# Delta rule: the products of the inverse's first levels as 64x64 blocks in two corners of the array, with their waits one projection matmul earlier

## The chip, the cores and the metric

The kernel runs on one core of a Trainium2 chip. The metric is the device time of one execution in microseconds (us), the median of a few runs. Before the change it is 1946.24 us over 3 runs (1946.16 to 1946.36).

## The reference

Two transformer blocks on a sequence of 512 positions with 2048 channels, in float32. The first block has three branches (a gated MLP with spatial gating, a gated delta rule, cross attention on a memory of 256 rows), the second has two attentions. What the change touches is the delta rule, which has 8 heads of 128 channels and works in chunks of 64 positions (8 chunks):

```
kb = k * beta;  vb = v * beta
a = where(strict, (kb k^T) * decay, 0)          # 64 x 64, strictly lower triangular, for each chunk
T = triangular_solve(a + eye, eye, lower, unit_diagonal)      # the inverse of (1 + a)
value = T vb;   k_cumdecay = T (kb * exp(g_cum))
...
then a scan over the chunks with a state of 128 x 128
```

## The kernel before

**Projections.** All large products are the same routine, `gemm` (line 1364): a tile of 128 output channels by 512 positions, accumulated over 16 blocks of 128 input channels. Each operand is split in a high and a low part, so each block takes three matmuls of 128x128 weights by 512 columns: high weights by high activations, high by low, low by high. ScalarE makes the high part of the weights (line 346), VectorE the low part (line 727), and the tile goes to one of two PSUM banks. SyncE loads the next weights. These matmuls follow each other on TensorE through the whole kernel.

**The delta rule beside them.** While TensorE works on the projections of head h, the chunk work of head h-1 is set between them. The order is written out by hand in `beside` (line 1601): `part(j, k0, k1)` issues blocks k0 to k1-1 of projection tile j, and between two parts stands one step of the delta rule. A Fori loop runs this for heads 1 to 7, and a copy after the loop does the last head beside the first gMLP tiles.

**The inverse.** T is built by doubling. Level 0 is done by VectorE alone. Level k, for k from 1 to 6, joins blocks of 2^k rows to blocks of 2^(k+1). A level is two products: `level_u` (line 1540) multiplies the masked matrix (ML, made by GpSimd in line 284) with the current inverse (XIE), and `level_w` (line 1553) multiplies the transposed inverse (YI) with the result (UI). Two pairs of chunks lie side by side, so that a tile of 128 partitions holds two chunks and each product is done for r = 0 and 1. At levels 1 to 5 each product is two calls of `mm` with 128x128 weights and 64 columns in float32, and each call shows as two weight loads and two matmuls. Everything in these tiles outside the blocks of 64x64 on the diagonal is zero or unused. Level 6 joins the two halves and is different: there `level_w` takes four calls, two of which have weights of 64 columns and write partitions 0 to 63 (line 1567).

**The chain of one level.** TensorE makes u in PSUM bank `pb[2]`; ScalarE copies it to UI (line 485, semaphore u_sb); TensorE makes w in `pb[3]`; VectorE adds it to the inverse (lines 1063 and 1064), adds two halves for the next u (line 1066, semaphore xy) and transposes for the next w (line 1068, semaphore yt). The products wait for these semaphores (lines 1542, 1543, 1555, 1557) right before their own matmuls. VectorE and ScalarE do this between their work for the projections of head h (convolution, line 921; SiLU, lines 359 to 361; weight splitting), each in one fixed order.

`pb[3]` is used before the heads for the gMLP statistics and transposes, and in the chunk scan by `kept_keys` (columns 128 to 255) and `chunk_out` (columns 0 to 127).

Of the kernel before, what the change touches and what calls it, by code (L numbers as in the profile page):

```python
# [12 lines left out]
P = 128  # L13
S = 512
D = 2048
KT = D // P
# [4 lines left out]
GM, DN, XA, MEM = 4, 8, 4, 256  # L21
# [9 lines left out]
U_DN = U_X + 2 * XA  # L31
U_ZU = U_DN + 4 * DN
# [14 lines left out]
LEVELS = 7  # L47
# [12 lines left out]
ACT = mybir.ActivationFunctionType  # L60
# [26 lines left out]
def build(nc, w, xT, memT, rows_in, consts, negatives, params, ws_t, bs_b, rel, x1_dram, rows_dram, outT):  # L87
    with ExitStack() as ctx:
# [28 lines left out]
        pb = [ctx.enter_context(nc.psum_tensor(f"pb{i}", [P, S], F32)) for i in range(6)]  # L117
# [16 lines left out]
        VB, QG, XI, YI, UI = (tl(i) for i in range(4, 9))  # L134
        XIE = UI[:, 2 * P:3 * P]
# [24 lines left out]
        def blk(a, c, n=1):  # L160
            return a[:, c * P:(c + n) * P]
# [28 lines left out]
        def packed(a, k):  # L190

            return a.rearrange("p (g b) -> p g b", b=1 << k)

        H = P // 2

        def v3(a):
            return a.rearrange("p (c t) -> p c t", t=P)
# [22 lines left out]
        sem = {n: ctx.enter_context(nc.semaphore(n)) for n in names}  # L220
# [113 lines left out]
        def _(act):  # L334
            st = Steps(act, sem["act_steps"])
            A = nc.scalar.activation
# [142 lines left out]
            def level(h, k):  # L479
                if k == LEVELS - 1:  # L480
                    act.wait_ge(sem["y_ps"], h + 1)
                    A(YI, pb[4][:, :], ACT.Copy)
                act.wait_ge(sem["u_ps"], (LEVELS - 1) * h + k)
                if k < LEVELS - 1:
                    A(UI[:, 0:P], pb[2][:, 0:P], ACT.Copy).then_inc(sem["u_sb"], 1)  # L485
                else:
                    A(UI[:, 0:P], pb[2][:, 0:P], ACT.Copy, scale=bits(C_ODD, k))
                    A(UI[:, P:2 * P], pb[2][:, 0:P], ACT.Copy, scale=bits(C_EVEN, k)).then_inc(sem["u_sb"], 1)
# [229 lines left out]
        def _(dve):  # L718
            st = Steps(dve, sem["dve_steps"])
            V = nc.vector  # L720
# [179 lines left out]
                    .then_inc(sem["sp_done"], 1)  # L900


            def dn_lo(h, j, quarters=range(4)):
                lo(4 * h + (U_DN + j + 2), (U_DN + j) % 2, quarters)

# [144 lines left out]
            def level(h, k):  # L1050

                n = LEVELS * h + (k + 1)
                if k == 0:
                    dve.wait_ge(sem["m_lvl"], n)
                    st.then(V.transpose(YI[:, 2 * P:4 * P], blk(ML, 0, 2)))
                    one = C["ident"].rearrange("p (c t) -> p c t", c=1).broadcast_to([P, 2, P])
                    V.scalar_tensor_tensor(v3(ordered(1)), v3(YI[:, 2 * P:4 * P]), bits(C_ODD, 0), one, ALU.mult, ALU.add)
                    st.then(V.scalar_tensor_tensor(v3(ordered(0)), v3(YI[:, 2 * P:4 * P]), bits(C_EVEN, 0), one, ALU.mult, ALU.add))
                else:
                    dve.wait_ge(sem["w_ps"], (LEVELS - 1) * h + k)  # L1060
                if 0 < k < LEVELS - 1:
                    w = packed(pb[3][:, 0:P], k)
                    V.scalar_tensor_tensor(blocks(k, 1, 0), w, bits(C_ODD, k), blocks(k, 1, 0), ALU.mult, ALU.add)
                    st.then(V.scalar_tensor_tensor(blocks(k, 0, 1), w, bits(C_EVEN, k), blocks(k, 0, 1), ALU.mult, ALU.add))
                if k < LEVELS - 1:
                    V.tensor_tensor(packed(XIE, k + 1), blocks(k + 1, 1, 0), blocks(k + 1, 0, 1), ALU.add).then_inc(sem["xy"], 1)
                    if k < LEVELS - 2:
                        V.transpose(YI[:, 0:2 * P], other_blocks(k + 1)).then_inc(sem["yt"], 1)
                else:
                    w = pb[4][:, 0:S // 2].rearrange("p (r two b) -> p r two b", two=2, b=H)  # L1070
                    for two, rows, cols in ((0, slice(0, H), slice(H, P)), (1, slice(H, P), slice(0, H))):
                        y = pair(YI, two)[rows, :, cols]
                        ins = V.tensor_tensor(y, y, w[rows, :, two, :], ALU.add)
                    ins.then_inc(sem["xy"], 1)
# [276 lines left out]
        def _(pe):  # L1351
            def mm(out, a, b, start=True, stop=True, skip=False):
                return nc.tensor.matmul(out, a, b, start=start, stop=stop, skip_group_check=skip)  # L1353
# [7 lines left out]
                mm(out, blk(a[0], i), b[1][:, cols], False, False)  # L1361
                return mm(out, blk(a[1], i), b[0][:, cols], False, True)

            def gemm(u, slot, k0=0, k1=KT, before=None, free=False):

                out = bank[slot][:, :]
                if k0 == 0:

                    pe.wait_ge(sem["evac"], u - 1)
                for k in range(k0, k1):  # L1370
                    if k % 4 == 0:
                        pe.wait_ge(sem["hi"], 4 * u + (k // 4 + 1))
                        pe.wait_ge(sem["lo"], 4 * u + (k // 4 + 1))
                    if before is not None:
                        pe.wait_ge(sem["act_hi"], before + k + 1)
                        pe.wait_ge(sem["act_lo"], before + k + 1)
                    ah, al = act_hi[:, k * S:(k + 1) * S], act_lo[:, k * S:(k + 1) * S]
                    wh, wl = w_hi[slot][:, k * P:(k + 1) * P], w_lo[slot][:, k * P:(k + 1) * P]
                    mm(out, wh, ah, k == 0, False)
                    mm(out, wh, al, False, False)  # L1380
                    ins = mm(out, wl, ah, False, k == KT - 1)
                    if free and k in (3, 7, 11):
                        ins.then_inc(sem["tiles"], 1)
                if k1 == KT:
                    ins.then_inc(sem["unit"], 1)
# [92 lines left out]
                mm(pb[0][:, :], sums[:, P:2 * P], NSH, True, False)  # L1478
                mm(pb[0][:, :], sums[:, P:2 * P], NSL, False, True).then_inc(sem["dn_ss"], 1)

            def dn_gemm(h, j, k0, k1):
                gemm(4 * h + (U_DN + j), (U_DN + j) % 2, k0, k1)

            dn_gemm(0, 0, 0, 1)
            for g in range(GM):
# [51 lines left out]
                    ins = tp(pb[1][:, c * P:(c + 1) * P], blk(VT, c))  # L1537
                ins.then_inc(sem["tp"], 1)

            def level_u(h, k):  # L1540

                pe.wait_ge(sem["m_lvl"], LEVELS * h + (k + 1))
                pe.wait_ge(sem["xy"], LEVELS * h + k)
                if k == LEVELS - 1:
                    for c in range(NB):
                        ins = tp(pb[4][:, c * P:(c + 1) * P], blk(XI, c // 2 + 2 * (c % 2 == 0)))
                    ins.then_inc(sem["y_ps"], 1)
                m = blk(ML, NB * (k % 2), 2)
                for r in range(2):
                    ins = mm(pb[2][:, r * H:(r + 1) * H], blk(m, r), XIE[:, r * H:(r + 1) * H])  # L1550
                ins.then_inc(sem["u_ps"], 1)

            def level_w(h, k):

                pe.wait_ge(sem["u_sb"], (LEVELS - 1) * h + k)
                if k < LEVELS - 1:
                    pe.wait_ge(sem["yt"], (LEVELS - 2) * h + k)
                    for r in range(2):
                        half = slice(r * H, (r + 1) * H)
                        ins = mm(pb[3][:, half], blk(YI, r), UI[:, half])  # L1560
                else:
                    for c in range(NB):
                        r, half = c // 2, slice(c * H, (c + 1) * H)
                        if c % 2:
                            ins = mm(pb[4][:, half], UI[:, (r + 1) * H:(r + 3) * H], YI[:, c * P:c * P + H])
                        else:
                            ins = mm(pb[4][0:H, half], UI[:, r * H:(r + 1) * H], YI[:, c * P + H:(c + 1) * P])
                ins.then_inc(sem["w_ps"], 1)
# [32 lines left out]
            def beside(part, p, h=None, late=0):  # L1601


                part(0, 0, 2)
                level_u(p, 1)
                part(0, 2, 5)
                level_w(p, 1)
                part(0, 5, 9)
                level_u(p, 2)
                part(0, 9, 13)  # L1610
                level_w(p, 2)
                part(0, 13, KT)
                for j in (1, 2):
                    part(j, 0, 1)
                    level_u(p, 2 * j + 1)
                    part(j, 1, 4)
                    level_w(p, 2 * j + 1)
                    if j == 1:
                        part(1, 4, 6)
                        transposes(p)  # L1620
                        part(1, 6, 9)
                    else:
                        part(2, 4, 9)
                    level_u(p, 2 * j + 2)
                    part(j, 9, 11 + j)
                    level_w(p, 2 * j + 2)
                    part(j, 11 + j, 14)
                    if h is not None:
                        norm_sum(h, j - 1)
                    part(j, 14, KT)  # L1630
# [22 lines left out]
            products(0)  # L1653
            dn_gemm(0, 3, 8, KT)
            with pe.Fori(1, DN) as h:
                beside(lambda j, k0, k1: dn_gemm(h, j, k0, k1), h - 1, h)
            beside(lambda j, k0, k1: gemm(U_ZU + j, (U_ZU + j) % 2, k0, k1), DN - 1, late=3)
            gemm(U_ZU + GM, U_ZU % 2, 0, 3)
            out_sum(DN - 1)
            gemm(U_ZU + GM, U_ZU % 2, 3, KT)  # L1660
# [182 lines left out]
```

## Time and profile before

| what | value |
|---|---|
| median of 3 runs | 1946.24 us |
| the profiled execution's own time | 1946.37 us |
| its span | 1944.7 us |
| TensorE matmul busy | 1928.7 us, 99% |
| TensorE weight load busy | 1599.7 us, 82% |
| VectorE busy | 1154.1 us, 59% |
| ScalarE busy | 815.0 us, 42% |
| GpSimd busy | 111.1 us, 6% |

The span is the time from the first to the last instruction that the profiler saw. PE is TensorE's matmuls and PEld its weight loads, which run beside the matmuls before them. A matmul is pipelined: its recorded length overlaps the next one, so the distance between the starts of two matmuls tells what one costs. The stretch with the heads' inverses is from about 285 to 743 us.

### The profile page before, as it was taken

How to read it: one execution, taken by the hardware profiler on the slowest of the kernel's cores; microseconds unless marked ns; L12 is line 12 of the kernel's file. 1: busy time of each engine (PE TensorE's matmuls, PEld its weight loads, DVE VectorE, ACT ScalarE, POOL GpSimd, SP SyncE). 2: the span in 40 equal slices, each digit the busy share in tenths (PEclk: the TensorE clock that was granted, in tenths of full speed). 3: DMA queues.
4: the chain of work that ended last, by engine and by line, in shares of the span. 5: the costliest groups of instructions: out<-in, count | busy, mean ns of one | idle time of the engine just before them, and what ended most of it. 6: DMA issues, size and time to landing. Idle time of an engine off the chain costs nothing.

```text
span 1944.7 us, 27615 instructions
## 1 busy us (share of the span) xinstructions
PE 1928.7 (99%) x9182; PEld 1599.7 (82%) x9182; DVE 1154.1 (59%) x2167; ACT 815.0 (42%) x1595; POOL 111.1 (6%) x170
## 2 busy tenths in 40 slices
PE   8999999999999999999999999999999999999999
PEld 6788788888888888888888888888888888888887
DVE  5655577887777865734465454646464646466332
ACT  5643344444454444523344343434343434344211
POOL 1100010111110110001000000000000000000010
PEclk9999999999999999999999999999999999999999
DMA  9622222322322312343322222222222222223341
GB/s 356 219 107 86 76 76 68 95 75 75 97 70 71 97 65 98 109 151 140 143 101 93 87 85 93 73 105 70 99 79 88 85 92 86 92 87 120 131 160 65
DMA packets 33402, 202.50 MB, mean 104 GB/s; under 512 B 4528, under 2 KB 4656, under 8 KB 12624
## 3 DMA queue, kind: packets, MB, share of 16 engines
q1 hardware_dynamic: 23616, 166.73, 23.9%
q0 software_dynamic: 9600, 35.10, 6.5%
q8 instruction: 27, 0.44, 0.1%
q10 hardware_dynamic: 144, 0.10, 0.0%
q14 instruction: 15, 0.12, 0.0%
HBM read 193.50 MB, written 8.42 MB: 104 GB/s over the span
## 4 chain that ended last, share of the span: by engine, by line
PE 94%; DMA 2%; DVE 2%; ACT 2%; issue 0%; SPq 0%; POOL 0%; DVEq 0%; ACTq 0%
PE gemm L1353 81%; PE pb L1353 10%; PE pb L1356 2%; DMA raw<-in_w 1%; DVE w_lo L727 0%; DVE act_lo L736 0%; ACT scratch L395 0%; DMA scratch<-in_rows_in 0%; ACT w_hi L346 0%; DMA scratch<-in_memT 0%; ACT act_hi L405 0%; DVE act_lo L749 0%; DVE scratch L921 0%; DVE w_lo L746 0%; ACT scratch L417 0%
## 5 line engine op out<-in xcount | busy, mean ns | idle before, releaser
L1353 PE MATMUL gemm<-act_lo,w_hi 128*128 128x512 f32 x2512 | 975.6, 391 | 7.7 <-DVE w_lo L727 4.7
L1353 PE MATMUL gemm<-act_hi,w_hi 128*128 128x512 f32 x2384 | 955.3, 401 | 1.2 <-DVE act_lo L758 1.1
L1353 PE MATMUL gemm<-act_hi,w_lo 128*128 128x512 f32 x2368 | 925.7, 391 | 0.0
L1353 PEld LDWEIGHTS gemm<-act_lo,w_hi 128*128 128x128 f32 x2512 | 473.2, 188 | 101.2 <-issue 11.4
L1353 PEld LDWEIGHTS gemm<-act_hi,w_hi 128*128 128x128 f32 x2384 | 448.8, 188 | 91.5 <-issue 8.1
L1353 PEld LDWEIGHTS gemm<-act_hi,w_lo 128*128 128x128 f32 x2368 | 444.7, 188 | 95.3
L346 ACT ACTIVATE w_hi<-raw 128x512 fp32r<-128x512 f32 x620 | 339.1, 619 | 409.9 <-PE gemm L1353 394.1
L727 DVE TENSOR_TENSOR w_lo<-raw,w_hi 128x512 fp32r<-128x512 f32 x620 | 396.5, 696 | 141.7 <-ACT w_hi L346 140.0
L1353 PEld LDWEIGHTS pb<-scratch 128*128 128x128 f32 (+1 forms) x892 | 129.0, 190 | 28.9 <-DVE scratch L1080 5.8
L1353 PE MATMUL pb<-scratch 128*128 128x128 f32 (+4 forms) x892 | 137.0, 280 | 2.0 <-DVE scratch L742 1.7
L1223 DVE SCALAR_TENSOR_TENSOR scratch<-gemm,scratch 128x512 f32<-128x512 f32 x24 | 16.6, 692 | 150.1 <-PE gemm L1353 149.9
L371 ACT ACTIVATE scratch<-pb,eps 128x512 f32<-128x512 f32 x42 | 29.0, 690 | 107.5 <-PE pb L1353 107.5
L359 ACT ACTIVATE scratch<-scratch 128x512 f32<-128x512 f32 x56 | 35.2, 628 | 89.2 <-DVE scratch L922 46.0
L284 POOL TENSOR_TENSOR scratch<-scratch,cst 128x256 f32<-128x256 f32 x56 | 47.5, 853 | 428.5 <-DVE scratch L971 255.7
L921 DVE SCALAR_TENSOR_TENSOR scratch<-scratch,par 128x511 f32<-128x511 f32 (+2 forms) x72 | 54.0, 750 | 9.8 <-DVE scratch L919 2.5
L611 ACT ACTIVATE scratch<-big 128x512 f32 (+1 forms) x16 | 10.1, 631 | 108.7 <-DVE big L1162 108.7
L1162 DVE TENSOR_TENSOR big<-gemm,scratch 128x512 f32 (+1 forms) x16 | 11.0, 687 | 68.3 <-PE gemm L1353 68.3
L1356 PEld LDWEIGHTS pb<-cst,scratch 128*128 128x128 f32 x380 | 44.8, 140 | 7.7 <-DVE scratch L892 0.6
L1356 PE MATMUL pb<-cst,scratch 128*128 128x128 f32 x380 | 50.7, 273 | 0.3 <-ACT scratch L548 0.3
L485 ACT ACTIVATE scratch<-pb 128x128 f32<-128x128 f32 x40 | 11.1, 277 | 91.0 <-PE pb L1353 90.5
L316 POOL DMA_DIRECT2D scratch<-in_rel x7 | 3.8, 539 | 662.1 <-DVE scratch L1275 662.1
L1353 PE MATMUL pb<-parts 128*128 128x384 f32 (+3 forms) x216 | 39.6, 331 | 0.0
(233 smaller groups left out, 1439.5 us busy)
## 6 DMA issues: line engine op xcount, KB each, us to landing
raw<-in_w SPq DMA_DIRECT2D x156, 1024.0 KB, 4.8
scratch<-in_rows_in POOLq DMA_DIRECT2D x6, 1024.0 KB, 7.9
big<-in_xT POOLq DMA_DIRECT2D x4, 1024.0 KB, 14.1
scratch<-rows POOLq DMA_DIRECT2D x16, 256.0 KB, 6.1
scratch<-in_xT POOLq DMA_DIRECT2D x16, 256.0 KB, 3.0
x<-big POOLq DMA_DIRECT2D x16, 256.0 KB, 2.3
scratch<-x POOLq DMA_DIRECT2D x16, 256.0 KB, 4.0
outT<-scratch POOLq DMA_DIRECT2D x16, 256.0 KB, 3.8
```

The source lines that it names most:

```text
L284: nc.gpsimd.tensor_tensor(v3(blk(ML, NB * (k % 2), 2)), pair(AT, 0), C[f"level{k}"].rearrange("p (c t) -> p c t", c=1).broadcast_to([P, 2, ...
L346: A(w_hi[slot][:, c], raw[slot][:, c], ACT.Copy).then_inc(sem["hi"], 1)
L359: st.then(A(E, SS, ACT.Exp, scale=-1.0))
L371: st.then(A(dst, src, ACT.Ln, bias=eps[:, 0:1], scale=scale))
L485: A(UI[:, 0:P], pb[2][:, 0:P], ACT.Copy).then_inc(sem["u_sb"], 1)
L611: A(SQ, x1, ACT.Square)
L727: V.tensor_tensor(w_lo[slot][:, c], raw[slot][:, c], w_hi[slot][:, c].bitcast(F32), ALU.subtract)\
L921: st.then(V.scalar_tensor_tensor(Y[:, 3 - k:], SS[:, :S - 3 + k], tap(k), Y[:, 3 - k:], ALU.mult, ALU.add))
L1162: V.tensor_tensor(x1, bank[u0 % 2][:, :], blk(XIN, NB * j, NB), ALU.add).then_inc(sem["evac"], 1)
L1223: V.scalar_tensor_tensor(dst, bank[slot(j)][:, :], SCALE if j == 0 else 1.0, R12, ALU.mult, ALU.mult)\
L1353: return nc.tensor.matmul(out, a, b, start=start, stop=stop, skip_group_check=skip)
L1356: return nc.tensor.transpose(out, a, C["ident"])
```

## The change

For levels 1 to 5, u and w are each made by four calls of `mm` in place of two. Each has weights of 64x64 and 32 columns: for each r one call on partitions 0 to 63 and one on partitions 64 to 127, which write the same partitions of PSUM. Together they write a quarter of what was written before (only the diagonal blocks), so the rest of the two areas is set to zero once by VectorE ahead of the heads. Both areas lie in `pb[3]`: u in columns 256 to 383 (it was in `pb[2]`), w in columns 384 to 511 (it was in columns 0 to 127). Level 6 keeps its matmuls and its u in `pb[2]`. The waits of all levels from 1 to 6 move out of `level_u` and `level_w` into `u_ready` and `w_ready`, which `gemm` calls before the last matmul of the part that precedes the level.

```
+        LU, LW = pb[3][:, 2 * P:3 * P], pb[3][:, 3 * P:4 * P]
+        def corner(r, half):
+            return slice(half * H, (half + 1) * H), slice(r * H + half * (H // 2), r * H + (half + 1) * (H // 2))
...
-                    A(UI[:, 0:P], pb[2][:, 0:P], ACT.Copy).then_inc(sem["u_sb"], 1)
+                    A(UI[:, 0:P], LU, ACT.Copy).then_inc(sem["u_sb"], 1)
...
+            V.memset(pb[3][:, 2 * P:4 * P], 0.0)
...
-                    w = packed(pb[3][:, 0:P], k)
+                    w = packed(LW, k)
...
-            def gemm(u, slot, k0=0, k1=KT, before=None, free=False):
+            def gemm(u, slot, k0=0, k1=KT, before=None, free=False, ready=None):
...
                     mm(out, wh, al, False, False)
+                    if ready and k == k1 - 1:
+                        ready()
                     ins = mm(out, wl, ah, False, k == KT - 1)
...
-            def level_u(h, k):
+            def u_ready(h, k):
                 pe.wait_ge(sem["m_lvl"], LEVELS * h + (k + 1))
                 pe.wait_ge(sem["xy"], LEVELS * h + k)
+            def w_ready(h, k):
+                pe.wait_ge(sem["u_sb"], (LEVELS - 1) * h + k)
+                if k < LEVELS - 1:
+                    pe.wait_ge(sem["yt"], (LEVELS - 2) * h + k)
+            def level_u(h, k):
                 if k == LEVELS - 1:
...
                 m = blk(ML, NB * (k % 2), 2)
                 for r in range(2):
-                    ins = mm(pb[2][:, r * H:(r + 1) * H], blk(m, r), XIE[:, r * H:(r + 1) * H])
+                    if k == LEVELS - 1:
+                        ins = mm(pb[2][:, r * H:(r + 1) * H], blk(m, r), XIE[:, r * H:(r + 1) * H])
+                    else:
+                        for half in range(2):
+                            p, c = corner(r, half)
+                            ins = mm(LU[p, c], blk(m, r)[p, p], XIE[p, c])
                 ins.then_inc(sem["u_ps"], 1)
             def level_w(h, k):
-                pe.wait_ge(sem["u_sb"], (LEVELS - 1) * h + k)
                 if k < LEVELS - 1:
-                    pe.wait_ge(sem["yt"], (LEVELS - 2) * h + k)
                     for r in range(2):
-                        half = slice(r * H, (r + 1) * H)
-                        ins = mm(pb[3][:, half], blk(YI, r), UI[:, half])
+                        for half in range(2):
+                            p, c = corner(r, half)
+                            ins = mm(LW[p, c], blk(YI, r)[p, p], UI[p, c])
...
             def beside(part, p, h=None, late=0):
-                part(0, 0, 2)
+                part(0, 0, 2, lambda: u_ready(p, 1))
                 level_u(p, 1)
-                part(0, 2, 5)
+                part(0, 2, 5, lambda: w_ready(p, 1))
                 level_w(p, 1)
...
```

The other calls of `part` that precede a level get the same argument.

## Rows read from the trace of the kernel before

**Rows 1.** The page: span, busy time by engine, clock by slice, the last chain.
```profile
span 1944.7 us, 27615 instructions
PE 1928.7 (99%) x9182; PEld 1599.7 (82%) x9182; DVE 1154.1 (59%) x2167; ACT 815.0 (42%) x1595; POOL 111.1 (6%) x170
...
PEclk9999999999999999999999999999999999999999
...
PE 94%; DMA 2%; DVE 2%; ACT 2%; issue 0%; SPq 0%; POOL 0%; DVEq 0%; ACTq 0%
```

**Rows 2.** Busy us (x instructions) by stretch: before, and with, the inverses.
```profile
237.00:285.00 48.00, 47.53 (x240) 39.81 (x239) 35.40 (x63) 21.29 (x37) 4.22 (x5) 1.00 0.27 75
285.00:743.00 458.00, 458.00 (x2410) 381.94 (x2409) 358.54 (x735) 210.83 (x413) 53.66 (x65) 1.00 0.27 77
```

**Rows 3.** Groups of TensorE by form: busy us, mean ns, idle before.
```profile
L1353 PE MATMUL pb<-scratch 128*128 128x64 f32 x384 | 55.6, 264 | 0.0
L1353 PE MATMUL pb<-scratch 128*64 128x64 f32 x32 | 5.3, 246 | 0.0
L1353 PEld LDWEIGHTS pb<-scratch 128*64 128x64 f32 x32 | 3.1, 134 | 3.4 <-issue 2.8
```

**Rows 4.** Timeline of TensorE's matmuls around one product: start, length in us.
```profile
640.00 0.40 PE L1353 MATMUL gemm<-act_hi,w_hi 128*128 128x512 f32 x1
640.24 0.39 PE L1353 MATMUL gemm<-act_lo,w_hi 128*128 128x512 f32 x1
640.47 0.39 PE L1353 MATMUL gemm<-act_hi,w_lo 128*128 128x512 f32 x1
640.70 0.55 PE L1353 MATMUL pb<-scratch 128*128 128x64 f32 x4
641.06 0.48 PE L1353 MATMUL gemm<-act_hi,w_hi 128*128 128x512 f32 x1
641.37 0.39 PE L1353 MATMUL gemm<-act_lo,w_hi 128*128 128x512 f32 x1
```

**Rows 5.** Timeline of the weight loads there; three in narrow windows.
```profile
640.47 0.64 PEld L1353 LDWEIGHTS pb<-scratch 128*128 128x128 f32 x4
640.70 0.19 PEld L1353 LDWEIGHTS pb<-scratch 128*128 128x128 f32 x1
640.81 0.19 PEld L1353 LDWEIGHTS pb<-scratch 128*128 128x128 f32 x1
640.92 0.19 PEld L1353 LDWEIGHTS pb<-scratch 128*128 128x128 f32 x1
641.03 0.19 PEld L1353 LDWEIGHTS gemm<-act_hi,w_hi 128*128 128x128 f32 x1
```

**Rows 6.** Timeline around level 6's w, narrow and wide weights in turn.
```profile
676.89 0.39 PE L1353 MATMUL gemm<-act_hi,w_lo 128*128 128x512 f32 x1
677.21 1.32 PE L1353 MATMUL pb<-scratch 128*64 128x64 f32 x8
...
678.65 0.39 PE L1353 MATMUL gemm<-act_lo,w_hi 128*128 128x512 f32 x1
```

**Rows 7.** Its weight loads in narrow windows, in order of time.
```profile
677.21 0.13 PEld L1353 LDWEIGHTS pb<-scratch 128*64 128x64 f32 x1 [0.35 <-issue]
677.21 0.19 PEld L1353 LDWEIGHTS pb<-scratch 128*64 128x64 f32 x2 [0.35 <-issue]
677.46 0.19 PEld L1353 LDWEIGHTS pb<-scratch 128*128 128x128 f32 x1
677.57 0.19 PEld L1353 LDWEIGHTS pb<-scratch 128*128 128x128 f32 x1
677.88 0.14 PEld L1353 LDWEIGHTS pb<-scratch 128*64 128x64 f32 x1
678.09 0.19 PEld L1353 LDWEIGHTS pb<-scratch 128*128 128x128 f32 x1
```

**Rows 8.** Timeline ahead of level 3's u: VectorE, then TensorE.
```profile
659.20 0.29 DVE L1066 TENSOR_TENSOR scratch<-scratch 128x128 f32<-128x128 f32 x1
659.93 0.39 PE L1353 MATMUL gemm<-act_hi,w_lo 128*128 128x512 f32 x1
660.16 0.55 PE L1353 MATMUL pb<-scratch 128*128 128x64 f32 x4
```

**Rows 9.** The copy of u, and the w that waits for it.
```profile
660.75 0.28 ACT L485 ACTIVATE scratch<-pb 128x128 f32<-128x128 f32 x1
662.69 0.55 PE L1353 MATMUL pb<-scratch 128*128 128x64 f32 x4
```

**Rows 10.** Timeline of VectorE where the new memset goes.
```profile
248.60 0.69 DVE L899 TENSOR_TENSOR big<-pb,scratch 128x512 f32<-128x512 f32 x1 [0.20 <-PE pb L1353]
249.21 0.68 DVE L913 TENSOR_TENSOR scratch<-gemm,scratch 128x512 f32<-128x512 f32 x1
...
260.67 0.42 DVE L943 SCALAR_TENSOR_TENSOR scratch<-scratch 128x256 f32<-128x256 f32 x1 [2.81 <-ACT scratch L372]
```

More of the change, by code:

```diff
@@ L1479, in norm_sum, with dn_gemm @@
                 mm(pb[0][:, :], sums[:, P:2 * P], NSL, False, True).then_inc(sem["dn_ss"], 1)
-            def dn_gemm(h, j, k0, k1):
-                gemm(4 * h + (U_DN + j), (U_DN + j) % 2, k0, k1)
+            def dn_gemm(h, j, k0, k1, ready=None):
+                gemm(4 * h + (U_DN + j), (U_DN + j) % 2, k0, k1, ready=ready)
             dn_gemm(0, 0, 0, 1)
@@ L1601, in beside @@
             def beside(part, p, h=None, late=0):
-                part(0, 0, 2)
+                part(0, 0, 2, lambda: u_ready(p, 1))
                 level_u(p, 1)
-                part(0, 2, 5)
+                part(0, 2, 5, lambda: w_ready(p, 1))
                 level_w(p, 1)
-                part(0, 5, 9)
+                part(0, 5, 9, lambda: u_ready(p, 2))
                 level_u(p, 2)
-                part(0, 9, 13)
+                part(0, 9, 13, lambda: w_ready(p, 2))
                 level_w(p, 2)
@@ L1613, in beside @@
                 for j in (1, 2):
-                    part(j, 0, 1)
+                    part(j, 0, 1, lambda: u_ready(p, 2 * j + 1))
                     level_u(p, 2 * j + 1)
-                    part(j, 1, 4)
+                    part(j, 1, 4, lambda: w_ready(p, 2 * j + 1))
                     level_w(p, 2 * j + 1)
@@ L1620, in beside @@
                         transposes(p)
-                        part(1, 6, 9)
+                        part(1, 6, 9, lambda: u_ready(p, 2 * j + 2))
                     else:
-                        part(2, 4, 9)
+                        part(2, 4, 9, lambda: u_ready(p, 2 * j + 2))
                     level_u(p, 2 * j + 2)
-                    part(j, 9, 11 + j)
+                    part(j, 9, 11 + j, lambda: w_ready(p, 2 * j + 2))
                     level_w(p, 2 * j + 2)
@@ L1655, in _ @@
             with pe.Fori(1, DN) as h:
-                beside(lambda j, k0, k1: dn_gemm(h, j, k0, k1), h - 1, h)
-            beside(lambda j, k0, k1: gemm(U_ZU + j, (U_ZU + j) % 2, k0, k1), DN - 1, late=3)
+                beside(lambda j, k0, k1, ready=None: dn_gemm(h, j, k0, k1, ready), h - 1, h)
+            beside(lambda j, k0, k1, ready=None: gemm(U_ZU + j, (U_ZU + j) % 2, k0, k1, ready=ready), DN - 1, late=3)
             gemm(U_ZU + GM, U_ZU % 2, 0, 3)
```

## The prediction

> **What bounds the kernel now.** I read the page first: matmuls are busy 1928.7 of 1944.7 us, the granted clock is full in all 40 slices, and 94% of the chain that ended last is TensorE's [rows 1]. A busy TensorE could still be a waiting one, so I took the stretches next: from 285 to 743 us, where all the inverses lie, it is busy 458.00 of 458.00 us, VectorE 358.54 and ScalarE 210.83 [rows 2]. Last I read the timeline around single products. So in this stretch the end is set by TensorE's own stream of instructions: whatever a product takes there is paid in full, and nothing is to be gained on the other engines. The question is only how much TensorE time one product of a level takes, in its old and its new form.
>
> **How many.** Levels 1 to 5, u and w, for 8 heads: 5 x 2 x 8 = 80 products change. The 384 matmuls of 64 columns with full weights [rows 3] fit: 80 x 4 = 320, and 8 x (4 + 4) = 64 belong to level 6, which keeps its form.
>
> **What an old product costs.** Projection matmuls follow each other every 0.23 us (640.00, 640.24, 640.47). From the last one before the product (640.47) to the second one after it (641.37) it is 0.90 us, in which 2 x 0.23 = 0.46 are the projections' own [rows 4]. The product takes 0.44 us. Its four weight loads start at 640.47, 640.70, 640.81 and 640.92, the projection's next at 641.03: 0.11 us for each load of 128 columns [rows 5]. 4 x 0.11 = 0.44, so a product is bound by its loads and the 64 columns that each matmul streams are hidden beneath them. The first load costs nothing extra, since it starts beneath the last projection matmul. I saw the same 0.90 to 0.91 us wherever I looked among the 80.
>
> **What a new product costs.** It has 8 loads of 64 columns and 8 matmuls of 32. The trace has no 64x64 weights. The nearest it has is level 6's w, with weights of 64 columns on all 128 rows, in turn with full ones [rows 3, 6, 7]. It tells three things.
> - *A load of 64 columns takes half:* two of them end 0.19 us after the first began, and one is 0.13 us long, so the second began 0.055 after the first [rows 7]. Eight in a row are 0.44 us: exactly the four old ones.
> - *Going from full to narrow weights stops the array.* The first narrow load does not start beneath the last projection matmul (676.89) but 0.32 us after its start [rows 6, 7], and the row names 0.35 us of idle time with nothing but issue ahead of it; 8 such entries make the 2.8 us [rows 3].
> - *Going back stops it too.* The narrow load at 677.88 would let the next load start 0.055 later; it starts at 678.09, 0.21 later [rows 7]. Taking 0.055 for the load and 0.055 for its matmul (two passes of 64 columns), 0.10 us pass with nothing in the array. No wait stands at this place, so it isn't the semaphore. The whole group checks this: 676.89 to 678.65 is 1.76 us [rows 6]; with 2 x 0.23 for projections and 4 x 0.11 + 4 x 0.055 for loads it would be 1.12. The excess of 0.64 over 4 switches is 0.16 us a switch.
>
> The Trainium skill says the same (TensorEngine Tiling (Array Packing), Tiling Modes, Key Properties): changing the tiling mode, not just the tile, drains TensorE. By that rule each of the 80 products, being alone between full-array matmuls, pays two drains; the trace agrees for the mode that it has.
>
> So a new product, from the start of the last projection matmul before it to the start of the second one after: 0.32 to its first load, L for its 8 loads, 0.03 for the last matmul (32 columns, half of 0.055), 0.10 until the array is empty, 0.11 for the projection's first load, which nothing hides now, and 0.235 to the second matmul (the load of a projection at 641.03 plus 0.11 gives 641.14, its second matmul is at 641.37). That is 0.795 + L, against 0.90.
>
> *L* lies between 0.22 (the two corners load fully beside each other, 4 x 0.055) and 0.44 (one after the other). The code issues two loads for one corner, then two for the other. A load is issued after the matmul before it, and in the rows the second load of a pair and its matmul stand 0.055 apart [rows 7]; with 32 columns the matmul can go 0.027 after its load begins. So I let the other corner's first load start 0.055 + 0.027 after this corner's first: 4 x 0.083 = 0.33. I take 0.33, the middle of the bounds.
>
> The Trainium skill (same page, Key Properties) has different tiles load and multiply in parallel, which would give L = 0.22; its Gotcha 1 has it that row tiles can't access the same PSUM bank at once, which speaks against it here, as both corners write `pb[3]`. No row of this trace can decide.
>
> The difference is 0.795 + 0.33 - 0.90 = 0.22 us, times 80 = 18 us. The bounds of L give 0.115 (9 us) and 0.335 (27 us). The array that must empty at the exit is only a corner, so the 0.10 may be half: 0.05 x 80 = 4 us less. I take 0.20 us a product: 16 us.
>
> **The other parts.**
> - *The waits one matmul ahead.* A wait that is met costs nothing at either place: the waiting load of a product starts 0.23 us before its matmul, as early as any other [rows 4, 5]. So moving them gives back nothing that is paid today, and the array must empty first in any case. What it can cost: queued behind the wait are the last low-weight matmul of the part and all of TensorE. The closest case is level 3's u: VectorE's add ends at 659.49, the product's matmul is at 660.16 [rows 8], its load 0.23 earlier at 659.93, and the matmul that carries the wait now has its load 0.23 earlier still, at 659.70. So 0.21 us are left there. The w after it has its copy done at 661.03 and begins at 662.69 [rows 9], 1.66 us. In the forecast each product lengthens TensorE's side and not VectorE's, which adds slack. Zero; bounds 0 and, if 0.2 us were missing in each of 8 heads, 2 us.
> - *ScalarE and VectorE* read the same 128x128 from another place of PSUM: the same time, beside TensorE.
> - *The memset* of 256 columns: some 0.4 us as other VectorE work of 256 columns (the 0.42 us at 260.67), ahead of a projection's evacuation at 249.21 that begins the moment that VectorE is free; VectorE later sits idle 2.81 us for ScalarE [rows 10]. Hidden; at most 0.4 us.
> - *More instructions*: 4 loads and 4 matmuls more for each product, 640 pairs. I count them in L.
>
> **Sum.** 1946.37 us, the profiled execution (span 1944.7 plus 1.7 around it), + 16 = 1962.4. The median of the runs shown is 0.13 lower. I forecast 1962 us; this case's own range is 1950 to 1974.
>
> **Rivals.**
> 1. *Corners do not stop the array* (ends on the other side). Then a product costs its loads alone: 0.33 in place of 0.44 us, -0.11 x 80 = -9 us, 1937 us; with L = 0.22, -18 us, 1929 us. In that case TensorE runs ahead of VectorE and the moved wait of level 3's u has less than its 0.21 us: the four products before it save 0.44 us, so up to 0.23 us in 7 heads, 2 us, are given back. For it: the trace shows the stop only for 128x64 weights. Against it: it shows it in both directions, 32 times. It decides if the two switches cost less than 0.11 us together; measured are 0.31. Chance 0.14.
> 2. *Neither a stop nor any overlap:* 8 x 0.055 = 4 x 0.11, 1946 us, no change. This is also the case where the form doesn't do what it says: two corners, but in turn. Chance 0.08.
> 3. *Stops, and the corners strictly in turn:* +0.335 x 80 = 27 us, 1973 us. For it: one bank of PSUM for both, and the order of issue. Chance 0.18.
> 4. *Stops, and full overlap with the short exit:* 0.115 - 0.05 = 0.065 us, 5 us, 1951 us. Chance 0.15.
> 5. *Moved waits that hold TensorE*, on top of any of these: at most 2 us, inside the ranges.
>
> The forecast itself has 0.45. Faster or slower by more than 0.2% (3.9 us, about what a measurement of this kernel can tell from no change): faster is rival 1, 0.14; same is rival 2 with a thin edge of the fourth, 0.09; slower is the rest, 0.77. The range 1945 to 1974 leaves out rival 1 and a little above the top.
>
> **What would show it.** In the timeline of the changed kernel, the first 64x64 load of a product should start some 0.32 us after the last projection matmul, not beneath it, with idle time put down to issue. Eight loads should then stand 0.055 apart where one corner follows itself, and closer where the corner changes; the projection's first load should come about 0.1 us after the last corner matmul's stream. From last projection matmul to the second after should be 1.05 to 1.25 us in all 80, and matmul busy should stay at the whole of the stretch, or show gaps put down to issue. The stretch should grow by 16 us and all the others by nothing. What would make it wrong: a first corner load that starts beneath the projection matmul (rival 1 or 2), or TensorE idle on line 1066 or 485.

## The result and the profile after

The changed kernel takes 1953.88 us (median of 6 runs, 1953.2 to 1954.91) against 1946.27 us (6 runs, 1946.06 to 1946.46): a ratio of 1.0039, 95% interval 1.0026 to 1.0052. It is 7.6 us slower. The forecast was 16 us slower: the sign and the stops at each product hold, the size is a factor of two too large, because one term of the sum, the time of a product's eight loads, was too long.

The page of the profiled execution, which was the slowest of the six (1954.91 us). The lines answer to [rows 1]:

```profile
span 1953.4 us, 28256 instructions
PE 1938.4 (99%) x9502; PEld 1585.9 (81%) x9502; DVE 1154.1 (59%) x2168; ACT 815.3 (42%) x1595; POOL 111.1 (6%) x170
...
PEclk8999999999999999999999999999999999999999
...
PE 94%; DMA 2%; DVE 2%; ACT 1%; issue 0%; SPq 0%; POOL 0%; DVEq 0%; ACTq 0%
```

320 weight loads and 320 matmuls were added, four and four for each of the 80 products, and one VectorE instruction (the memset). Weight load busy went *down*. By stretch, cut at about the same places of the program as in [rows 2] (columns: span; busy us and count for matmuls, weight loads, VectorE, ScalarE, GpSimd; granted clock; DMA share; GB/s):

```profile
0.00:238.00 238.00, 228.51 (x1027) 183.04 (x1028) 129.30 (x229) 115.93 (x229) 14.19 (x28) 0.98 0.47 172
238.00:286.00 48.00, 47.53 (x240) 39.79 (x240) 35.63 (x64) 21.30 (x37) 4.22 (x5) 1.00 0.25 74
286.00:752.00 466.00, 466.00 (x2732) 365.29 (x2731) 358.83 (x736) 211.04 (x413) 53.65 (x65) 1.00 0.26 76
```

The stretch with the inverses grew from 458 to 466 us, and TensorE is busy in all of it, before and after. The first stretch is 1.0 us longer, at a granted clock of 0.98 where the kernel before had 1.00. That belongs to this execution and not to the change: the program is the same there, and the other five executions have a mean granted clock of 0.999 against its 0.997, and spans of 1951.7 to 1952.5 us. It is why this span grew by 8.7 us and the median by 7.6. The memset adds nothing: in its stretch TensorE does 240 matmuls in 47.53 busy us as before.

One product, TensorE's matmuls by time (start, length), which answers to [rows 4]:

```profile
646.94 0.39 PE L1360 MATMUL gemm<-act_lo,w_hi 128*128 128x512 f32 x1
647.17 0.39 PE L1360 MATMUL gemm<-act_hi,w_lo 128*128 128x512 f32 x1
647.49 0.42 PE L1360 MATMUL pb<-scratch 64*64 64x32 f32 x8
647.84 0.50 PE L1360 MATMUL gemm<-act_hi,w_hi 128*128 128x512 f32 x1
648.18 0.39 PE L1360 MATMUL gemm<-act_lo,w_hi 128*128 128x512 f32 x1
```

From 647.17 to 648.18 it is 1.01 us; it was 0.90. Read in the same way, all 80 products lie within 0.01 us of these values, and their sum goes from 72.6 to 80.8 us: 8.2 us, the whole loss. The first corner matmul stands 0.32 us after the last projection matmul in place of 0.23. The weight loads of the same product, the first two lines below from a window of a few ns at its beginning, the third from the whole (against [rows 5]):

```profile
647.48 0.13 PEld L1360 LDWEIGHTS pb<-scratch 64*64 64x64 f32 x1 [0.35 <-issue]
647.48 0.14 PEld L1360 LDWEIGHTS pb<-scratch 64*64 64x64 f32 x2 [0.35 <-issue]
647.48 0.31 PEld L1360 LDWEIGHTS pb<-scratch 64*64 64x64 f32 x8 [0.35 <-issue]
647.84 0.19 PEld L1360 LDWEIGHTS gemm<-act_hi,w_hi 128*128 128x128 f32 x1
```

Two loads together end 0.14 us after the first began and one alone is 0.13 long: the second starts less than 0.01 us after the first. In [rows 7] two loads for the same half took 0.19. So the corners load side by side, all eight loads are over in 0.31 us, and ahead of them stands idle time put down to issue, which means that the profile shows nothing that the loads waited for. By form, in the whole program, it comes 80 times (28.3 / 0.35):

```profile
L1360 PEld LDWEIGHTS pb<-scratch 64*64 64x64 f32 x640 | 24.9, 133 | 28.3 <-issue 28.3
L1360 PEld LDWEIGHTS pb<-scratch 128*64 128x64 f32 x32 | 3.1, 135 | 3.4 <-issue 2.8
```

### The profile page after: what moved, and what is told of

It reads as the page before. It is cut to its first block, busy times and chain, and to the rows that moved or that the text cites. A ratio compares the mean times of both kernels' runs of the same rounds, so it can differ in the third digit from the quotient of the medians.

```text
span 1953.4 us, 28256 instructions
## 1 busy us (share of the span) xinstructions
PE 1938.4 (99%) x9502; PEld 1585.9 (81%) x9502; DVE 1154.1 (59%) x2168; ACT 815.3 (42%) x1595; POOL 111.1 (6%) x170
## 4 chain that ended last, share of the span: by engine, by line
PE 94%; DMA 2%; DVE 2%; ACT 1%; issue 0%; SPq 0%; POOL 0%; DVEq 0%; ACTq 0%
PE gemm L1360 82%; PE pb L1360 10%; PE pb L1363 2%; DMA raw<-in_w 1%; DMA scratch<-in_rows_in 1%; DVE w_lo L732 0%; DVE act_lo L741 0%; ACT w_hi L351 0%; DMA scratch<-in_memT 0%; ACT scratch L400 0%; DVE act_lo L754 0%; ACT act_hi L410 0%; DVE scratch L928 0%; DVE w_lo L751 0%; ACT scratch L422 0%
## 5 line engine op out<-in xcount | busy, mean ns | idle before, releaser
L1360 PEld LDWEIGHTS pb<-scratch 64*64 64x64 f32 (+2 forms) x1212 | 105.7, 160 | 50.6 <-issue 31.1
L1360 PE MATMUL pb<-scratch 64*64 64x32 f32 (+5 forms) x1212 | 125.8, 255 | 2.0 <-DVE scratch L747 1.7
```

## The experiments

I call the array cut when the weights take a half or a corner of it, and a run of such products between full-array ones a visit, with an entry and an exit. A pair of loads below is one load in each corner, side by side. The theory after this look: a visit stops TensorE at a fixed price, which each of the 80 products pays alone; the two corners then load fully beside each other. The first rival: the moved waits are part of the loss.

**Only the waits moved.** From the changed kernel, the products (in place of the calls by corner) and their PSUM areas set back, `u_ready` and `w_ready` kept:

```
-        LU, LW = pb[3][:, 2 * P:3 * P], pb[3][:, 3 * P:4 * P]
+        LU, LW = pb[2][:, 0:P], pb[3][:, 0:P]
...
-            V.memset(pb[3][:, 2 * P:4 * P], 0.0)
...
+                    ins = mm(pb[2][:, r * H:(r + 1) * H], blk(m, r), XIE[:, r * H:(r + 1) * H])
...
+                        ins = mm(LW[:, half], blk(YI, r), UI[:, half])
```

> The kernel before, with only the waits of the levels moved one projection matmul ahead; the products keep 128x128 weights. Theory (the loss is the array's two stops at each product of 64x64 blocks, and the moved waits cost and bring nothing): 1946.3 us, within 1 us of before, a product still takes 0.90 to 0.91 us from last projection matmul to the second after. Rival (part of the loss is the moved waits, which hold TensorE for VectorE, above all at level 3's u): 1947 to 1949 us, with TensorE idle put down to the line of the add for xy. A third reading (the moved waits bring time and hide some of the loss): below 1945 us.

Measured: 1946.35 us (11 runs) against 1946.33, ratio 0.9999 (0.999 to 1.0008). The products still take 0.90 to 0.91 us, all but one. There, at level 3's u of one head, the projection's load that now carries the wait starts late, after VectorE's add for xy:

```profile
422.58 0.29 DVE L1072 TENSOR_TENSOR scratch<-scratch 128x128 f32<-128x128 f32 x1
422.99 0.19 PEld L1359 LDWEIGHTS gemm<-act_hi,w_lo 128*128 128x128 f32 x1 [0.33 <-issue]
```

The add ends at 422.87, the load starts 0.12 later, and TensorE loses 0.17 us in all. The profile puts the idle time down to issue; that it is the moved wait is read from its place and from the add's end. The moved waits bring nothing, and cost too little for the medians to show, with full-array products. The other half, corners with their waits right before them, wasn't tried.

**One corner left out.** `for half in range(1)` in both products: half of the loads and matmuls, with the visits unchanged (half of the blocks are not computed).

> The changed kernel with the calls of the second corner (half = 1) left out at levels 1 to 5, so half of the inverse's blocks are not computed. Theory (the two corners load and multiply fully beside each other, L = 0.22 us for either number of corners): 1953.5 us, at most 1 us below the changed kernel; the first load of a product still 0.32 us after the last projection matmul. Rival (the corners partly share something: loads, issue, the one PSUM bank): 80 x 0.03 to 0.11 us less, 1945 to 1951 us.

Measured: 1953.2 us (5 runs), ratio 1.0036 (1.0023 to 1.0049). One of its products, matmuls:

```profile
588.22 0.39 PE L1360 MATMUL gemm<-act_hi,w_lo 128*128 128x512 f32 x1
588.53 0.41 PE L1360 MATMUL pb<-scratch 64*64 64x32 f32 x4
588.88 0.50 PE L1360 MATMUL gemm<-act_hi,w_hi 128*128 128x512 f32 x1
589.22 0.39 PE L1360 MATMUL gemm<-act_lo,w_hi 128*128 128x512 f32 x1
```

1.00 us in place of 1.01. The second corner is nearly free: at most 0.01 us a product, and 0.7 us in the medians. The loads, by form, say the same: 320 loads of one corner are busy for 24.3 us, the 640 of both were for 24.9.

```profile
L1360 PEld LDWEIGHTS pb<-scratch 64*64 64x64 f32 x320 | 24.3, 133 | 28.3 <-issue 28.3
```

The forecast's L, the time of the eight loads, is refuted here: with corners that hold each other up, this kernel would have been 80 x 0.11 = 9 us faster than the changed one.

**Each product twice in one visit.** `for half in (0, 1, 0, 1)`.

> The changed kernel with each product of levels 1 to 5 issued twice within the same visit to 64x64 blocks (16 loads in place of 8; the second writes the same values again). Theory (two stops at a fixed price for each visit, and 0.055 us for each load of one corner with the other corner free beside it): +4 x 0.055 = 0.22 us a product, 80 x 0.22 = 18 us more than the changed kernel, 1971 us. Rival (the cost lies in the number of instructions, not in the visit: (0.90 + 0.10 - 0.46) / 8 = 0.068 us for each of the 8 pairs): +0.54 us a product, 43 us, 1997 us.

Measured: 1972.4 us (4 runs), ratio 1.0135 (1.0119 to 1.015), 18.5 us over the changed kernel, where 18 were expected and the rival had 43.

```profile
599.27 0.39 PE L1360 MATMUL gemm<-act_hi,w_lo 128*128 128x512 f32 x1
599.59 0.66 PE L1360 MATMUL pb<-scratch 64*64 64x32 f32 x16
600.17 0.50 PE L1360 MATMUL gemm<-act_hi,w_hi 128*128 128x512 f32 x1
600.51 0.39 PE L1360 MATMUL gemm<-act_lo,w_hi 128*128 128x512 f32 x1
```

1.24 us: 0.23 more for eight more loads, 0.058 for each pair of loads in the two corners. The entry is 0.32 as before.

**Corner by corner.** The loops of a product turned round, so that four loads for one corner are issued before the first for the other:

```
-                for r in range(2):
...
-                        for half in range(2):
+                    for half in range(2):
+                        for r in range(2):
                             p, c = corner(r, half)
```

> The changed kernel with the loops of a product turned round: both calls of the first corner, then both of the second, in place of alternating corners call by call. Theory A (TensorE takes loads out of order for whichever corner is free, far enough ahead to see past four pairs): 1954 us, unchanged, loads in pairs a few ns apart as before. Theory B (it looks ahead only as far as the next call): the first corner's second call holds up the other corner, L rises from 0.22 to 0.33 or 0.44 us, 80 x 0.11 to 0.22 = 9 to 18 us more, 1963 to 1972 us.

Measured: 1953.86 us (5 runs), level with the changed kernel's 1953.88; two loads from a narrow window at the beginning, then all eight:

```profile
586.93 0.14 PEld L1360 LDWEIGHTS pb<-scratch 64*64 64x64 f32 x2 [0.36 <-issue]
586.93 0.32 PEld L1360 LDWEIGHTS pb<-scratch 64*64 64x64 f32 x8 [0.36 <-issue]
```

0.32 us in place of 0.31. One after the other they would take four times 0.058 more. Two loads start within some 0.01 us of each other again, where two of one corner stand 0.055 to 0.058 apart, so the second is the other corner's. TensorE looks past four loads, with their matmuls, of one corner, and starts the other's first load ahead of the last three of them.

**One call.** `for half in range(1 - r)`: a quarter of the work of a product, two loads (the rest is not computed).

> The changed kernel with only one of the four calls left in each product of levels 1 to 5 (r = 0, first corner), so three quarters of the inverse's blocks are not computed. Theory (0.058 us for each load of a corner, on top of a fixed price for the visit): from the run with one corner, which takes 1.00 us, 2 x 0.058 less, 0.885 us; 80 x 0.116 = 9 us less, 1944 us: with a quarter of the work, still no more than 2 us below the kernel before. Rival (the price of the visit depends on what is in it, for example the weights must be loaded twice before the array may go back): 1948 us or more.

Measured: 1944.59 us (10 runs), ratio 0.999 (0.9981 to 1.0).

```profile
580.75 0.39 PE L1360 MATMUL gemm<-act_hi,w_lo 128*128 128x512 f32 x1
581.07 0.30 PE L1360 MATMUL pb<-scratch 64*64 64x32 f32 x2
581.30 0.50 PE L1360 MATMUL gemm<-act_hi,w_hi 128*128 128x512 f32 x1
581.64 0.39 PE L1360 MATMUL gemm<-act_lo,w_hi 128*128 128x512 f32 x1
```

0.89 us, against 0.90 for the full product of before. With 2, 4 and 8 loads in a corner (this run, the run with one corner, the doubled one) a product takes 0.89, 1.00 and 1.24 us. A line through the three has 0.058 a load (the second corner's loads add at most 0.01), on 0.77 for an empty visit, which no run has. Two projection matmuls are 0.46 of that. So a visit costs 0.31 us, the same for 2, 4 and 8 loads in a corner. In this run, whose products are the shortest, the moved waits do hold TensorE: at level 3's u of two heads by 0.26 and 0.47 us (as read above), and one of these is named in TensorE's waits (in total, times, longest):

```profile
PE gemm L1360 <- DVE scratch L1073: 0.2, 1, 0.2
```

L1073 is the add for xy. Without these two the run would be 0.7 us shorter.

**Columns cut only.** Weights of 128 rows and 64 columns: `blk(m, r)[:, p], XIE[:, c]` and the same for w.

> The changed kernel with the array cut in columns only: at levels 1 to 5 the weights are 128x64 (all rows, 64 columns) and the calls stream the 32 columns on all 128 partitions; the result is the same since the blocks off the diagonal are zero. Theory A (any cut of the array costs two stops, and two column halves load beside each other): about the changed kernel, 1954 us, perhaps 2 us more as the stream must pass all rows at the exit. Theory B (the halves are only independent where the rows differ too): 8 loads in a row, L = 0.44, 80 x 0.22 = 18 us more, 1972 us.

Measured: 1953.6 us (5 runs), ratio 1.0038 (1.0024 to 1.0051). The loads of one product, and all by form (32 of them are level 6's):

```profile
586.54 0.31 PEld L1360 LDWEIGHTS pb<-scratch 128*64 128x64 f32 x8 [0.35 <-issue]
L1360 PEld LDWEIGHTS pb<-scratch 128*64 128x64 f32 x672 | 28.2, 136 | 31.6 <-issue 31.1
```

Eight loads in 0.31 us, and 672 in 28.2 us of busy time: they overlap as the corners do. Cutting the rows adds nothing, neither to the price nor to the gain.

**Level 6 without a cut array.** If changing mode is what costs, the kernel before pays for it four times in each level 6 [rows 6]. Two runs on the kernel before, of which only `level_w`'s narrow call is changed:

```
-  ins = mm(pb[4][0:H, half],  UI[:, r * H:(r + 1) * H],  YI[:, c * P + H:(c + 1) * P])
+  ins = mm(pb[4][:, half],    UI[:, r * H:r * H + P],    YI[:, c * P + H:(c + 1) * P])     # 128 columns
+  ins = mm(pb[4][0:72, half], UI[:, r * H:r * H + 72],   YI[:, c * P + H:(c + 1) * P])     # 72 columns
```

> The kernel before, with only level 6's w changed: its two calls with weights of 64 columns get 128 columns (the 64 more rows of output are not read), so that the whole array is used throughout and nothing changes mode. Theory (a change of mode costs 0.16 us, 4 of them at each level 6): the group goes from 1.76 us to 0.46 + 8 x 0.11 = 1.35 us, 0.41 us x 8 heads = 3.3 us less, 1943.0 us. Rival (the gaps around the narrow weights come from narrow weights or from the wait, not from changing mode): the four wider loads cost 4 x 0.055 x 8 = 1.8 us more, 1948 us.

> As the run before, but with 72 columns of weights in place of 128: more than 64, so that the instruction still uses the whole array. Theory (mode costs 0.16 us a change, a load costs by its columns, 72 x 0.86 ns = 0.062 us): the group takes 0.46 + 4 x 0.11 + 4 x 0.062 = 1.15 us, 0.61 x 8 = 4.9 us less than before, 1941.4 us. Rival (narrow weights as such stop the array, whatever the mode): no change, 1946 us.

Measured: 1943.09 us (11 runs; ratio 0.9985, 0.9976 to 0.9994) and 1941.97 us (11 runs; 0.9979, 0.997 to 0.9988) against 1946.05. *Wider* weights made the kernel faster. With 128 columns the group runs through without a stop, and takes 1.35 us to the second projection matmul behind it (557.16 to 558.51), as worked out, in place of 1.76:

```profile
557.16 0.39 PE L1353 MATMUL gemm<-act_hi,w_lo 128*128 128x512 f32 x1
557.38 1.00 PE L1353 MATMUL pb<-scratch 128*128 128x64 f32 x8
558.51 0.39 PE L1353 MATMUL gemm<-act_lo,w_hi 128*128 128x512 f32 x1
```

The matmuls with 72 columns, and three weight loads in a row, two of 72 columns and a full one, from a narrow window:

```profile
557.07 0.39 PE L1353 MATMUL gemm<-act_hi,w_lo 128*128 128x512 f32 x1
557.30 0.86 PE L1353 MATMUL pb<-scratch 128*72 128x64 f32 x8
557.96 0.48 PE L1353 MATMUL gemm<-act_hi,w_hi 128*128 128x512 f32 x1
558.28 0.39 PE L1353 MATMUL gemm<-act_lo,w_hi 128*128 128x512 f32 x1
557.58 0.32 PEld L1353 LDWEIGHTS pb<-scratch 128*72 128x72 f32 x3
```

The group follows the projection by 0.23 us, without a stop, and takes 1.21 us from 557.07 to 558.28 in place of 1.76. I expected 1.15, and the loads are not why it is more. The third load of the window is a full one, 0.19 long, so it starts 0.32 - 0.19 = 0.13 after the first: 0.065 for each load of 72 columns, about the 0.062 that I had worked out. But the group's first load hides beneath the projection matmul, and in its place the projection's own full load behind the group is paid. The group pays three loads of 72 columns and five full ones: 0.46 + 3 x 0.065 + 5 x 0.11 = 1.21.

**Level 6 in one visit.** The opposite way on the same place: all four calls with 64 columns, alternating halves of the array, two stops in place of four.

```
-  ins = mm(pb[4][:, half],    UI[:, (r + 1) * H:(r + 3) * H], YI[:, c * P:c * P + H])
+  ins = mm(pb[4][H:P, half],  UI[:, (r + 2) * H:(r + 3) * H], YI[:, c * P:c * P + H])
```

> The kernel before, with only level 6's w changed: all four calls have weights of 64 columns, two that write partitions 0 to 63 and two that write 64 to 127, so that the group is one visit to the array cut in columns in place of two (2 stops in place of 4), and its loads stand beside each other. Theory (a visit costs its two stops, and pairs of loads in different halves 0.058 us together): 0.32 + 4 x 0.058 + 0.06 + 0.10 + 0.11 + 0.235 = 1.05 us against 1.76, 0.71 x 8 = 5.7 us less than before, 1940.4 us, and 1 to 1.5 us below the run with 72 columns. Rival (the halves do not load beside each other when they stream 64 columns): 4 x 0.055 us more in each group, 1942.2 us, level with the run of 72 columns.

Measured: 1940.54 us (7 runs) against 1946.25, ratio 0.9969 (0.9958 to 0.9981): the best of all, 5.7 us below the kernel before and 13 below the changed one.

```profile
555.87 0.39 PE L1353 MATMUL gemm<-act_hi,w_lo 128*128 128x512 f32 x1
556.19 0.45 PE L1353 MATMUL pb<-scratch 128*64 128x64 f32 x8
556.57 0.50 PE L1353 MATMUL gemm<-act_hi,w_hi 128*128 128x512 f32 x1
556.91 0.39 PE L1353 MATMUL gemm<-act_lo,w_hi 128*128 128x512 f32 x1
```

1.04 us a group, as worked out (1.05).

## Why the prediction was right, and where not

The direction, the number of products and the two stops were right. The time of a product's eight loads was wrong, and makes the factor of two.

*What bounds the kernel; 80 products; 0.11 us a load of before.* Right. The 458 us grew to 466, all in TensorE's own stream, and the other stretches did not move but for the start of one execution. Two counts were wrong, and stand in no sum: 320 loads and 320 matmuls were added, not 640 pairs, and the four calls write half of the two areas and not a quarter; a quarter is what is left of the multiplications. The text gives its range once from 1950 and once from 1945 us; 1953.88 lies in both.

*Two stops a product.* Right, and taken from level 6's rows: the entry is 0.32 us as there, and the exit is that of [rows 7] too. Going by the loads, the last of eight begins some 0.13 us before 647.79, is in after 0.055, streams 0.03, and 0.10 us later, at 647.84, the projection's load begins. I had let the exit be up to half as long as only a corner must empty, and took 0.02 us (2 us in all) off the sum for it. It is not shorter, and where the weights fill all 128 rows (columns cut only) the product takes the same 1.01 us.

*L, the eight loads: the step that failed.* I took 0.33 us, since a load would wait for the matmul issued before it, and put 0.083 between the corners. Measured are 0.23 (4 x 0.058): the other corner's first load starts within 0.01 us, ahead of the first corner's second load, which is issued before it, and even an order of four loads for one corner first costs nothing. With L = 0.23 the working of the forecast gives 0.795 + 0.23 - 0.90 = 0.12, and the trace shows 1.01 - 0.90 = 0.10 to 0.11; 80 x 0.10 = 8 us, where the medians differ by 7.6. So of the 0.20 us forecast for a product, 0.10 was this term. That the rest fits so well is in part luck: the 0.02 us taken off for a shorter exit was not there, but the other terms together came out 0.02 shorter than I had them.

The bound of 9 us was in the text, from the rows (4 x 0.055). I gave it, with a short exit, 0.15, and the middle of the two bounds 0.45. The wait that gave the middle was one that no row showed. The rule of the Trainium skill (TensorEngine Tiling (Array Packing), Tiling Modes, Key Properties) that tiles load and multiply in parallel holds here, as these numbers show. The rule that I set against it (same page, Gotcha 1, row tiles and one PSUM bank) did not bite: both corners write `pb[3]`, on different partitions, and the second one costs 0.01 us.

*The waits cost nothing.* Right for the changed kernel: in its trace no projection matmul ahead of a product is held, and no wait of TensorE names the add for xy or the copy of u. Elsewhere level 3's u was held, once with the old products (0.17 us, waits only) and twice with the shortest (0.7 us, one call). The 0.21 us of [rows 8] were not the least: at another head of the kernel before,

```profile
422.81 0.29 DVE L1066 TENSOR_TENSOR scratch<-scratch 128x128 f32<-128x128 f32 x1
423.21 0.39 PE L1353 MATMUL gemm<-act_hi,w_lo 128*128 128x512 f32 x1
```

the add ends at 423.10, and the load that would carry the wait starts at 422.98, 0.12 us before. In the changed kernel the longer products hide this. The place of [rows 8] in the changed kernel (timeline, VectorE and TensorE, against [rows 8]):

```profile
666.13 0.29 DVE L1073 TENSOR_TENSOR scratch<-scratch 128x128 f32<-128x128 f32 x1
667.20 0.40 PE L1360 MATMUL gemm<-act_hi,w_lo 128*128 128x512 f32 x1
667.52 0.42 PE L1360 MATMUL pb<-scratch 64*64 64x32 f32 x8
```

The add ends at 666.42, and the matmul that carries the wait, at 667.20, has its load 0.23 earlier, at 666.97: 0.55 us are left, 0.34 more than the 0.21 that I had worked out; the four longer products before it (4 x 0.10 us) give VectorE that time. The smallest such distance among the heads is 0.42 us. *The memset* is hidden: right.

*Rivals.* No stop at all (0.14), and neither a stop nor any overlap (0.08): refuted by 80 idle times put down to issue. Corners in turn (0.18): refuted by one corner and by the doubled product. Full overlap with the short exit (0.15, 1951 us): the overlap was true, the short exit was not, and the time lies between this rival and the forecast.

## What to carry to other kernels

Small products that stand alone between full-array matmuls did not gain from a cut array: here each visit cost 0.31 us, a pair of 64-column loads in two halves then 0.058, against 0.11 for each full load in the whole array. Where each full load becomes a pair, as here, that is even at 0.31 / (0.11 - 0.058), by this estimate about 6 full loads in one visit, and a product has 4. The runs lie on both sides of it: 1.01 us against 0.90 with four full loads, and 1.24 (the doubled product) against 1.35 (level 6's w with 128 columns) with eight. Where two half-used full loads become one pair, as in level 6's w, the same estimate is 0.31 / (0.11 - 0.029), about 4, and it has 8. And where a kernel goes back and forth between weights of 64 and of 128 columns, either widen the narrow ones (72 and 128 were tried) or gather them in one visit. The price is known here for float32, in a chain that TensorE bounds, on one core; of matmuls of other lengths or types around the visit no run tells.

## What was not expected of the hardware

TensorE took a load for the free corner ahead of three loads, with their matmuls, issued earlier for the other (eight loads in 0.32 us in that order, 0.31 in the alternating one). Halves that share all rows and differ only in columns load beside each other as diagonal corners do (1953.6 and 1953.88 us). Weights of 72 columns ran without any stop, at some 0.065 us a load, while those of 64 columns stopped TensorE on the way in and out.
